# Two transformer layers and a second block on one core: five reordered places and attention scores one unit ahead

## The chip, the cores and the metric

The kernel runs on one core of one Trainium2 chip, in one launch. The metric is the device time in microseconds (us); the median of three runs is taken. The engines are PE (products), DVE (vector), ACT (activations), POOL and SP, of which the last issues nearly all DMAs. Each has a queue of its own, worked in order; they meet at semaphores.

## The reference

One sequence of 256 tokens, model width 1024, fp32, goes through two layers (`first_block`) and a second block:

```python
for l in range(DEPTH):                       # 2
    mod = silu(c) @ w_ada[l] + b_ada[l]      # 1024 x 6144: sh1, sc1, gt1, sh2, sc2, gt2
    h = x * (1.0 + sc1) + sh1
    z = h @ w_in[l] + b_in[l]                # split in aq ak av | bq bk bv bf | cq ck cv cg | gates
    ya = rmsnorm(diff_attention(aq, ak, av, lam))       # A: 4 heads, two softmax maps each
    yb = forgetting_attention(bq, bk, bv, log_sigmoid(bf))   # B: 4 heads
    yc = groupnorm(retention(rotary(cq), rotary(ck), cv)) * silu(cg)   # C: 4 heads
    m = ga * (ya @ w_pa) + gb * (yb @ w_pb) + gc * (yc @ w_pc)
    x = layernorm(ALPHA * x + gt1 * (m @ w_out[l]))
    h = x * (1.0 + sc2) + sh2
    u, g = split(h @ w_up[l])                # 2 x 2816
    x = layernorm(ALPHA * x + gt2 * ((gelu(conv3(u)) * g) @ w_down[l]))
```

The second block (the middle and the expert loop) is a gated delta rule, a SwiGLU, a windowed attention and a mixture of 8 experts of which each token takes 2, each with a residual and a layer norm.

## The kernel before

Every fp32 product is three products of parts: each operand is split in a high part (ACT rounds it, L1482) and a low part (DVE subtracts it, in place, L1871), and `product` issues high x high (L794), low (L795) and high x low (L796). Weights come in slots of 1 MB (128 x 2048) through a ring of four slots `W` that SP fills (L653). `RING_LOADS` lists them by part of the program (layer0, layer1, middle); slot numbers start at 0 in each part. A slot is free when PE has used its low part and, for the high part, there are two slots, so `high(n)` on ACT and `low(n)` on DVE mean: split the next n half-weights. Where they stand in each engine's program sets the order of the work.

The results of PE go to the eight PSUM banks (each 2 KB a partition), handed out as a ring in the order of the jobs (`psum`); a job starts when the one eight places earlier has been copied out. `take_chunk` on DVE copies a finished chunk of z with its bias (L1861), and frees its bank.

The modulation `mod` is made in twelve chunks of 512 columns (`ada`): DVE multiplies weight rows by silu(c) and adds them in 8 steps (L1937, L1939), PE adds the 128 partitions with a product by a matrix of ones (`ada_column`, L922, one column for 128; `ada_row`) and DVE adds the bias (`ada_in`, L2004). Chunks 0 to 3 of layer 0 are made ahead of the first product, chunks 4 to 9 within the six chunks A0 to B2 of z, and 10 and 11 and the chunks of the next layer in `up`, one step (L1964) a tile. `ada_column(c)` waits for the chunk's sum.

A layer runs: hT (transposes of x, scale and shift, split: `shifted`/`high_shifted`), chunks A0 to A2, B0 to B2 and bf, then C and the gates as `background` pieces of the attention loops. There are eight units of A (u = 0 to 7) and eight of B (8 to 15): PE makes the scores (`attend`), DVE masks them and takes the maximum (`mask`, L2139, L2142), ACT the exponentials (L1542), DVE the probabilities (L2312 to L2318), PE transposes them (`attend_T`, L968) and multiplies by v (`attend_out`). Four C heads follow. The mixer's outputs: transposes of yA and yB, products pa and pb, transposes of yC, pc, the gated sum `mix`, its transposes mT, the product with w_out, residual and norm (L2047), then up (22 tiles of 128 hidden columns; the width-3 convolution by three operations, L2119 to L2123, Gelu on ACT, L1576, the gate L2099 and the split L2101 and L2103) and down. After down, the last norm of a layer waits for the split of the next layer's first weights (`high_next`).

## Time and profile before

| | us |
|---|---|
| median of 3 runs | 3078.68 |
| lowest and highest | 3076.17, 3080.14 |
| profiled execution, whole | 3081.78 |
| its span in the trace | 3080.0 |
| layer 0, layer 1 | 0 to 712, 712 to 1364 |
| middle, expert loop | 1364 to 2040, 2040 to 3080 |

The profiled execution is 3.1 us above the median of the runs, 1.8 us of which lie outside its span. In the profile's rows the first number is the start in us from the start of the span, the second the duration in us; "x32" are 32 instructions in one row, and "[9.85 <-DVE arena L1861]" says that the engine stood idle for 9.85 us before it and what ended that. An fp32 product shows as more than one instruction (passes). The mean granted clock of PE is 0.919 of its full speed.

### The profile page before, as it was taken

Reading aid. Unit: us, or ns where it says so; the run is one execution under the profiler, and the core shown is the slowest. Engines: PE = TensorE matmul, PEld = TensorE weight load, DVE = VectorE, ACT = ScalarE, POOL = GpSimd, SP = SyncE. Lnnn points to the kernel's source line nnn. Section 1 sums busy time; section 2 is a strip of 40 time slices with the busy share of each in tenths; the row PEclk is TensorE's granted clock in tenths of the full one; section 3 lists DMA queues with packets and bytes.
Section 4 is the critical chain, followed back from the end, with each engine's and each line's share of the span. In section 5 each row is a group of like instructions: output and inputs, shape, how many; then the busy total and the mean of one; then the engine's idle time right before and its main releaser. Section 6 shows DMA issues by size and latency. Waiting matters only on the chain.

```text
span 3080.0 us, 38153 instructions
## 1 busy us (share of the span) xinstructions
PE 2696.3 (88%) x13946; PEld 2285.4 (74%) x13946; DVE 2236.1 (73%) x2873; ACT 1470.6 (48%) x1685; POOL 24.0 (1%) x46
## 2 busy tenths in 40 slices
PE   4888888996888779968889996769999999999997
PEld 3667768875666669858788975658888888888885
DVE  6766668868656759745576646469889898898987
ACT  2233433323244333325334324447777777777774
POOL 0000000000000000000000000000000000000000
PEclk7889989998899889978999987669999999999998
DMA  7733435566433345432205552239899898898985
GB/s 303 261 130 127 140 137 202 209 239 250 186 135 127 123 165 213 161 113 108 69 15 177 189 207 108 85 121 361 340 350 356 339 367 338 339 362 343 369 338 214
DMA packets 104569, 671.11 MB, mean 218 GB/s; under 512 B 11968, under 2 KB 12096, under 8 KB 26992
## 3 DMA queue, kind: packets, MB, share of 16 engines
q1 hardware_dynamic: 97440, 622.08, 54.1%
q0 software_dynamic: 6992, 47.19, 4.1%
q8 instruction: 87, 1.43, 0.2%
q14 instruction: 50, 0.41, 0.0%
HBM read 665.03 MB, written 4.19 MB: 217 GB/s over the span
## 4 chain that ended last, share of the span: by engine, by line
PE 43%; DVE 24%; PEld 17%; issue 8%; ACT 6%; DMA 2%; PEldq 0%; DVEq 0%; SPq 0%; ACTq 0%
PE bank L794 12%; PE bank L795 12%; PE bank L796 12%; DVE W_low L1871 8%; PEld bank L796 6%; PEld bank L794 5%; PEld bank L795 5%; PE bank L1136 3%; DVE work L1939 2%; ACT W_high L1482 2%; DMA W<-in_w_expert 1%; ACT scores L1542 1%; PE bank L851 1%; PEld bank L1366 1%; DVE arena L1964 1%
## 5 line engine op out<-in xcount | busy, mean ns | idle before, releaser
L1871 DVE TENSOR_TENSOR W_low<-W,W_high 128x1024 fp32r<-128x1024 f32 x426 | 496.0, 1207 | 328.3 <-ACT W_high L1482 321.6
L1482 ACT ACTIVATE W_high<-W 128x1024 fp32r<-128x1024 f32 x426 | 422.1, 1039 | 588.3 <-PE bank L796 284.3
L795 PE MATMUL bank<-W_low,arena_parts 128*128 128x512 f32 x1224 | 482.8, 394 | 0.0
L794 PE MATMUL bank<-W_high,arena_parts 128*128 128x512 f32 x904 | 364.9, 404 | 30.1 <-DVE work L2467 19.8
L796 PE MATMUL bank<-W_high,arena_parts 128*128 128x512 f32 x904 | 358.4, 396 | 0.0
L796 PE MATMUL bank<-hT_high,W_low 128*128 128x256 f32 x1184 | 341.0, 288 | 0.0
L794 PE MATMUL bank<-W_high,hT_high 128*128 128x512 f32 (+3 forms) x744 | 304.2, 409 | 39.7 <-DVE arena L1861 20.9
L794 PE MATMUL bank<-hT_high,W_high 128*128 128x256 f32 x1072 | 312.3, 291 | 11.6 <-DVE arena L1861 8.8
L795 PE MATMUL bank<-W_low,hT_high 128*128 128x512 f32 (+4 forms) x784 | 310.3, 396 | 0.0
L795 PE MATMUL bank<-hT_low,W_high 128*128 128x256 f32 x1072 | 307.3, 287 | 0.0
L796 PE MATMUL bank<-W_high,hT_low 128*128 128x512 f32 (+3 forms) x744 | 294.1, 395 | 0.0
L794 PE MATMUL bank<-arena_parts 128*128 128x512 f32 x672 | 272.4, 405 | 1.9 <-DVE arena_parts L2979 1.9
L795 PEld LDWEIGHTS bank<-W_low,arena_parts 128*128 128x128 f32 x1224 | 233.4, 191 | 47.6
L796 PE MATMUL bank<-arena_parts 128*128 128x512 f32 x672 | 263.5, 392 | 0.0
L796 PEld LDWEIGHTS bank<-hT_high,W_low 128*128 128x128 f32 x1184 | 233.7, 197 | 0.0
L794 PEld LDWEIGHTS bank<-W_high,arena_parts 128*128 128x128 f32 x904 | 173.6, 192 | 69.9 <-issue 22.0
L795 PE MATMUL bank<-arena_parts 128*128 128x512 f32 x576 | 225.2, 391 | 0.0
L1528 ACT ACTIVATE arena_parts<-W 128x2048 fp32r<-128x2048 f32 x96 | 184.3, 1920 | 84.3 <-DMA W<-in_w_expert 66.2
L794 PEld LDWEIGHTS bank<-hT_high,W_high 128*128 128x128 f32 x1072 | 209.7, 196 | 16.4 <-issue 10.9
L1904 DVE TENSOR_TENSOR W_low<-W,arena_parts 128x2048 fp32r<-128x2048 f32 x96 | 217.9, 2283 | 3.4 <-ACT arena_parts L1528 3.4
L795 PEld LDWEIGHTS bank<-hT_low,W_high 128*128 128x128 f32 x1072 | 210.0, 196 | 0.5 <-issue 0.5
L794 PEld LDWEIGHTS bank<-W_high,hT_high 128*128 128x128 f32 x744 | 152.3, 205 | 76.5 <-issue 42.2
(372 smaller groups left out, 4719.1 us busy)
## 6 DMA issues: line engine op xcount, KB each, us to landing
W<-in_w_expert SPq DMA_DIRECT2D x192, 1024.0 KB, 4.8
W<-in_w_layer SPq DMA_DIRECT2D x170, 1024.0 KB, 4.9
arena<-in_w_expert SPq DMA_DIRECT2D x144, 1024.0 KB, 4.8
W<-in_w_middle SPq DMA_DIRECT2D x58, 1024.0 KB, 4.8
arena<-in_w_layer POOLq DMA_DIRECT2D x40, 1024.0 KB, 6.9
R<-in_rows_layer SPq DMA_DIRECT2D x70, 256.0 KB, 6.2
R<-in_rows_middle SPq DMA_DIRECT2D x18, 256.0 KB, 5.8
spread<-arena POOLq DMA_DIRECT2D x1, 3072.0 KB, 12.8
```

Source lines behind the costliest of these rows:

```text
L794: mm(bank, lhs[0], rhs[0], start=start, stop=False)
L795: mm(bank, lhs[0], rhs[1], start=False, stop=False)
L796: return mm(bank, lhs[1], rhs[0], start=False, stop=stop)
L851: last = turn_over(bank[:, i * P:(i + 1) * P], src[:, t, f:f + P], ident)
L1136: last = mm(bank[:, i * P:(i + 1) * P], lhs(i), rhs(i), start=True, stop=True)
L1366: last = turn_over(bank[:, i * P:(i + 1) * P], hid_tok[:, c % 2, i * P:(i + 1) * P], ident)
L1482: do(high_slot(at, w)[:, cols], raw(at, w)[:, cols], ACT.Copy).then_inc(main_highs.filled[main_highs.slot(at, w)], 1)
L1528: do(expert_high(j), expert_raw(j), ACT.Copy).then_inc(stream.raised, 1)
L1542: i = do(scores[:, b, m, 0:K], scores[:, b, m, 0:K], ACT.Exp, bias=nmax[:, b, m:m + 1], accum_out=rsum[:, b, m:m + 1])
L1871: tt(lows(at, w)[:, cols], raw(at, w)[:, cols], high_slot(at, w)[:, cols].bitcast(F32), ALU.subtract).then_inc(*low_ready.event(at))
L1904: tt(expert_low(j), expert_raw(j), expert_high(j).bitcast(F32), ALU.subtract).then_inc(stream.lowered, 1)
L1939: i = stt(acc, part, csil[:, f:f + 1], acc, ALU.mult, ALU.add)
```

## The change

Nothing of what is computed changes, but chunks 0 to 3 of `mod` are made in another way. Six parts:

- **Launch** (layer 0): `ada_first` multiplies the four chunks on PE directly, weight columns stationary, silu(c) moving; two before the transposes of x and two after; DVE only adds. The constants are loaded in two parts, x two weights later, and the two halves of `shifted` have a weight split between them.
- **Sums**: `first_steps` makes the steps of chunks 4 to 9 a generator. Of a chunk's eight steps three stand ahead of `take_chunk`, three (five at A0) behind; the others behind bf and in units 0 to 3 of A. Double steps in `up` are from tile 15 on, and the first column sum of the next layer moves from up's tile 21 to down's first.
- **Attention**: PE's scores, DVE's mask and ACT's exponentials of unit u+1 stand ahead of the probabilities of u.
- **Mixer outputs**: transposes and splits of yA and yB move into the C stage (their buffers from hT to the arena). Order of the products: pa0, pa1, pb0, yC's transposes, pb1, pc0, first half of pc1, first half of mT, rest of pc1, rest of mT, out. `mix` is signalled by tile, not once.
- **Ring slots**: `RING_START` lets the next part go on with the slot after the last one.
- **Convolution**: the first tap is an ACT Identity with scale and bias, the high part of the hidden a copy by ACT, the bank is freed by the gate of j-1, the low part of j-2 comes behind it.

In the middle, splits are moved from between the halves of a residual to behind the shift (and expert slots behind the last one). The counts of `high` and `low` follow. The core of the diff:

```diff
+RING_START = {part: sum(len(RING_LOADS[p]) for p in list(RING_LOADS)[:n]) for n, part in enumerate(RING_LOADS)}
...
-        yATs = hT_high[:, 0:4, :], hT_low[:, 0:4, :]
-        yBTs = hT_high[:, 4:8, :], hT_low[:, 4:8, :]
+        yATs, yBTs = both(7680, 9224, 4, S), both(2048, 3072, 4, S)
...
+            def more_constants():
+                sp.wait_ge(consts_in, 16)
+                sp.dma_start(consts[:, 2 * P:], ins["constants"][:, 2 * P:]).then_inc(consts_in, 16)
...
+                load_all(at, after, None if l else {("ada", 1, 1): first_inputs, ("A", 1, 1): more_constants})
...
-                        pool.wait_ge(*ada_ready.nth(at, 3))
+                        pool.wait_ge(*weights.full(at, ("A", 0, 0)))
...
+            def ada_first(c):
+                pe.wait_ge(*psum.vacant(at, ("ada", c)))
+                bank = banks[psum.slot(at, ("ada", c))]
+                for half in range(2):
+                    w = ("ada", c, half)
+                    pe.wait_ge(*weights.full(at, w))
+                    part = W[:, weights.slot(at, w), :]
+                    for i in range(4):
+                        n = 4 * half + i
+                        for k in range(4):
+                            f = 4 * half + k
+                            a_ = k * 512 + i * P
+                            last = mm(bank[:, n:n + 1], part[:, a_:a_ + P], csil[:, f:f + 1], start=k == 0, stop=k == 3)
+                    if half == 0:
+                        last.then_inc(*weights.frees(at, w))
+                last.then_inc(*psum.fills(at, ("ada", c)))
+                used.append((w, ("ada", c)))
+                hand_back()
...
+                    for c in range(2):
+                        ada_first(c)
...
                     transposes("hT", x, KD, None, 0)
-                    for c in range(4):
-                        ada_column(c)
+                    for c in range(2, 4):
+                        ada_first(c)
                 for n in range(6):
                     kind, c = ("A", n) if n < 3 else ("B", n - 3)
                     run(chunk((kind, c), (kind, c), hTs, KD, 512, 0 if n == 0 else None))
-                    if n:
+                    if n in (1, 3, 4, 5):
                         hand_back()
-                        (ada_row if n < 3 else ada_column)(3 + n)
+                        {1: ada_row, 3: ada_row}.get(n, ada_column)({1: 4, 3: 5, 4: 6, 5: 7}[n])
...
+                scores_a(0)
                 for h_ in range(A_HEADS):
                     for t in range(NT):
-                        attend("A", h_, t, aT[:, h_, :], aT[:, 4 + h_, :], 2)
+                        if u < 7:
+                            scores_a(u + 1)
                         next(bg)
+                        if u == 4:
+                            hand_back()
+                            ada_column(9)
                         attend_T("A", h_, t, u, 1)
...
                 transposes("cT", zCqk, 8, None, 0)
+                transposes("yA", yA, 4, y_ready, 1)
...
+                    if h_ == 1:
+                        transposes("yB", yB, 4, y_ready, 3)
                 for _ in bg:
                     pass
-                transposes("yA", yA, 4, y_ready, 1)
-                transposes("yB", yB, 4, y_ready, 3)
-                for b, (yT, kt) in enumerate(((yATs, 4), (yBTs, 4), (yCTs, 8))):
-                    if b == 2:
-                        transposes("yC", yC, 8, y_ready, 5)
-                    for n in range(2):
-                        run(chunk(("p", b, n), ("p" + "abc"[b], n), yT, kt, 512,
-                                  None if n else (4, 6, 8)[b]))
-                transposes("mT", mix, KD, h_ready, 1, 0)
+                for n in range(2):
+                    run(chunk(("p", 0, n), ("pa", n), yATs, 4, 512, None if n else 4))
+                run(chunk(("p", 1, 0), ("pb", 0), yBTs, 4, 512, 6))
+                transposes("yC", yC, 8, y_ready, 5)
+                run(chunk(("p", 1, 1), ("pb", 1), yBTs, 4, 512))
+                run(chunk(("p", 2, 0), ("pc", 0), yCTs, 8, 512, 8))
+                c = chunk(("p", 2, 1), ("pc", 1), yCTs, 8, 512)
+                next(c)
+                transposes("mT", mix, KD, h_ready, 1, 1, NT, quarters=(0,))
+                run(c)
+                transposes("mT", mix, KD, h_ready, 1, 1, NT, quarters=(1,))
                 for n in range(2):
                     run(chunk(("out", n), ("out", n), mixTs, KD, 512, None if n else 12))
-                transposes("h2T", x, KD, h_ready, 2, 1, NT)
+                transposes("h2T", x, KD, h_ready, 5, 1, NT)
...
-                    if j == 21 and l + 1 < DEPTH:
-                        hand_back()
-                        next_column(0)
                 def between_down(c):
-                    if l + 1 < DEPTH and c in (3, 6, 8):
+                    if l + 1 < DEPTH and c in (0, 3, 6, 8):
...
+            def hidden_conv(n, hid, taps):
+                def copy(j):
+                    act.wait_ge(*hid_mul.nth(a.at, j + 1))
+                    do(hid[0][:, j, :], acted[:, j % 2, :], ACT.Copy).then_inc(*hid_high.event(a.at))
+                for j in range(n):
+                    act.wait_ge(*psum.full(a.at, ("up", j)))
+                    bank = banks[psum.slot(a.at, ("up", j))]
+                    c = work[:, (j % 2) * S:(j % 2 + 1) * S]
+                    do(c, bank[:, 0:S], ACT.Identity, scale=taps[:, 2 * n + j:2 * n + j + 1],
+                       bias=taps[:, 3 * n + j:3 * n + j + 1]).then_inc(*hid_tap.event(a.at))
+                    high(1)
+                    if j:
+                        copy(j - 1)
+                    act.wait_ge(*hid_pre.nth(a.at, j + 1))
+                    if j >= 2:
+                        act.wait_ge(*hid_ready.nth(a.at, j - 1))
+                    do(acted[:, j % 2, :], c, ACT.Gelu).then_inc(*hid_act.event(a.at))
+                    act.wait_ge(*hid_act.last(a.at))
+                copy(n - 1)
...
+                    high_shifted("hT", 8, 0, lambda q: high(1))
...
+            def first_steps():
+                for c in range(4, 10):
+                    acc = work[:, c % 2 * 512:c % 2 * 512 + 512]
+                    if c > 5:
+                        dve.wait_ge(*psum.full(v.at, ("ada", c - 2)))
+                    for f in range(KD):
+                        w = ("ada", c, f // 4)
+                        if f % 4 == 0:
+                            dve.wait_ge(*adas.full(v.at, w))
+                        part = ada_slots[:, adas.slot(v.at, w), f % 4 * 512:(f % 4 + 1) * 512]
+                        if f == 0:
+                            i = ts(acc, part, csil[:, 0:1], None, ALU.mult)
+                        else:
+                            i = stt(acc, part, csil[:, f:f + 1], acc, ALU.mult, ALU.add)
+                        i.then_inc(dve_done, 1)
+                        dve.wait_ge(dve_done, v.count())
+                        if f % 4 == 3:
+                            dve.nop().then_inc(*adas.frees(v.at, w))
+                        if f == KD - 1:
+                            dve.nop().then_inc(*ada_ready.event(v.at))
+                        yield
...
+                if c < 4:
+                    tt(m, bank[:, 4:8], m, ALU.add).then_inc(dve_done, 1)
+                    dve.wait_ge(dve_done, v.count())
...
+                def gate(j):
+                    dve.wait_ge(*hid_act.nth(v.at, j + 1))
+                    bank = banks[psum.slot(v.at, ("up", j))]
+                    whole = acted[:, j % 2, :]
+                    tt(whole, whole, bank[:, S:2 * S], ALU.mult).then_inc(*hid_mul.event(v.at))
+                    dve.wait_ge(*hid_mul.last(v.at))
+                    dve.nop().then_inc(*psum.frees(v.at, ("up", j)))
+                def rest(j):
+                    dve.wait_ge(*hid_high.nth(v.at, j + 1))
+                    tt(hid[1][:, j, :], acted[:, j % 2, :], hid[0][:, j, :].bitcast(F32), ALU.subtract
+                       ).then_inc(*hid_ready.event(v.at))
+                    dve.wait_ge(*hid_ready.last(v.at))
                 for j in range(n):
-                    dve.wait_ge(*psum.full(v.at, ("up", j)))
+                    low(1)
+                    dve.wait_ge(*hid_tap.nth(v.at, j + 1))
                     u = banks[psum.slot(v.at, ("up", j))]
                     c = work[:, (j % 2) * S:(j % 2 + 1) * S]
-                    low(1)
-                    ts(c, u[:, 0:S], taps[:, 2 * n + j:2 * n + j + 1], taps[:, 3 * n + j:3 * n + j + 1], ALU.mult, ALU.add).then_inc(dve_done, 1)
-                    dve.wait_ge(dve_done, v.count())
                     stt(c[:, 1:S], u[:, 0:S - 1], taps[:, n + j:n + j + 1], c[:, 1:S], ALU.mult, ALU.add).then_inc(dve_done, 1)
                     dve.wait_ge(dve_done, v.count())
                     stt(c[:, 2:S], u[:, 0:S - 2], taps[:, j:j + 1], c[:, 2:S], ALU.mult, ALU.add).then_inc(*hid_pre.event(v.at))
                     dve.wait_ge(*hid_pre.last(v.at))
                     if j:
-                        finish_hidden(j - 1, hid, True)
+                        gate(j - 1)
+                    if j > 1:
+                        rest(j - 2)
                     between(j)
-                finish_hidden(n - 1, hid, True)
+                gate(n - 1)
+                rest(n - 2)
+                rest(n - 1)
...
                     low(1)
-                    ada(4 + n, 0)
+                    sums(3)
                     low(1)
-                    ada(4 + n, 1)
                     take_chunk(kind, c, lambda t: z[:, t, c * 512:(c + 1) * 512], ready)
-                    if n:
-                        ada_in(3 + n)
+                    if n in (1, 3, 4, 5):
+                        ada_in({1: 4, 3: 5, 4: 6, 5: 7}[n])
+                    sums(3 if n else 5)
...
+                mask_a(0)
                 for u in range(8):
                     h_, t = divmod(u, NT)
                     K, b = (t + 1) * P, u % 2
-                    mask("A", h_, t, u, 2, A_DQK ** -0.5, lambda m, K: blocks[:, 2 * P - K:2 * P])
+                    if u < 7:
+                        mask_a(u + 1)
                     dve.wait_ge(*exped.nth(v.at, u + 1))
...
+                    if u < 4:
+                        sums(2)
                     if u == 2:
                         log_forget()
+                    if u == 4:
+                        fold(32, 40, 16, 24, 64)
...
+                dve.wait_ge(*gate_done.nth(v.at, 2))
+                for n in range(2):
+                    gated(0, n)
+                low_tiles("yC", 2, yCTs)
+                low(1)
+                dve.wait_ge(*gate_done.nth(v.at, 3))
+                gated(1, 0)
+                low(1)
+                gated(1, 1)
+                low(1)
+                dve.wait_ge(*gate_done.nth(v.at, 4))
+                gated(2, 0, h_ready)
+                low(1)
+                low_tiles("mT", 1, mixTs)
+                low(1)
+                gated(2, 1, h_ready)
+                low_tiles("mT", 2, mixTs, 1)
+                low(1)
                 low(2)
                 residual(outs("out")[0:2], 0, ALPHA)
-                low(2)
+                low(1)
...
                 residual(outs("out")[2:4], 0, ALPHA)
                 norm(h_ready)
-                shifted("h2T", modc[:, 64:72], modc[:, 72:80])
+                shifted("h2T", modc[:, 64:72], modc[:, 72:80], lambda q: low(q))
...
-                    for _ in range(2 if j > 9 and j % 2 else 1):
+                    for _ in range(2 if j > 13 and j % 2 else 1):
...
             residual(outs("gout")[0:2], None, ALPHA)
-            low(2)
+            low(1)
             residual(outs("gout")[2:4], None, ALPHA)
             norm(h_ready)
-            shifted("fxT", modc[:, 0:8], modc[:, 8:16])
+            shifted("fxT", modc[:, 0:8], modc[:, 8:16], lambda q: low(q))
...
             low(1)
-            lower_slot(0, 1)
-            lower_slot(0, 2)
             residual(outs("wout")[2:4], None, ALPHA)
             norm(h_ready)
             shifted("mxT", modc[:, 32:40], modc[:, 40:48])
+            lower_slot(0, 1)
+            lower_slot(0, 2)
```

## Rows read from the trace of the kernel before

**Rows 1.** Part 1 of the page: busy us (share of span) x instructions.

```profile
PE 2696.3 (88%) x13946; PEld 2285.4 (74%) x13946; DVE 2236.1 (73%) x2873; ACT 1470.6 (48%) x1685; POOL 24.0 (1%) x46
```

**Rows 2.** PE's waits over the span: total us, times, longest us.

```profile
PE bank L851 <- DVE x L2047: 79.0, 7, 20.4
PE bank L794 <- DVE arena L1861: 29.7, 6, 9.8
...
PE bank L968 <- DVE scores L2318: 25.3, 12, 4.7
...
PE bank L968 <- DVE small L2385: 19.1, 8, 4.8
```

**Rows 3.** Timeline of PE at launch: start, us, engine, line, operation [idle before <-releaser].

```profile
19.50 0.95 PE L922 MATMUL bank<-consts,work 128*128 128x1 f32 x8
28.24 1.87 PE L922 MATMUL bank<-consts,work 128*128 128x1 f32 x8 [7.79 <-DVEq L1947]
...
50.99 0.76 PE L794 MATMUL bank<-W_high,hT_high 128*128 128x512 f32 x1 [7.76 <-DVE hT_low L1898]
```

**Rows 4.** Timeline of DVE at launch: seven of the eight sum operations.

```profile
7.00 5.59 DVE L1939 SCALAR_TENSOR_TENSOR work<-W,small,work 128x512 f32<-128x512 f32 x7
```

**Rows 5.** Timeline of PE in the middle: products of one column.

```profile
1437.82 5.53 PE L1171 MATMUL bank<-consts,arena 128*128 128x1 f32 x32 [0.33 <-PE bank L796]
```

**Rows 6.** Timeline of PE, layer 0, chunk bf: 4-column products (48 in a row).

```profile
142.18 0.25 PE L794 MATMUL bank<-W_high,hT_high 128*128 128x4 f32 x1
...
142.49 0.35 PE L796 MATMUL bank<-W_high,hT_low 128*128 128x4 f32 x1
```

**Rows 7.** Timeline of DVE, layer 1, chunk B0.

```profile
772.93 2.36 DVE L1871 TENSOR_TENSOR W_low<-W,W_high 128x1024 fp32r<-128x1024 f32 x2
775.21 3.10 DVE L1939 SCALAR_TENSOR_TENSOR work<-arena,small,work 128x512 f32<-128x512 f32 x4
778.64 1.53 DVE L1861 TENSOR_TENSOR arena<-bank,R 128x512 f32<-128x512 f32 x2 [0.32 <-DVE work L1939]
```

**Rows 8.** Timeline of PE, layer 1, behind chunk B0.

```profile
779.47 0.77 PE L794 MATMUL bank<-W_high,hT_high 128*128 128x512 f32 x1 [9.85 <-DVE arena L1861]
```

**Rows 9.** Timeline of PE, layer 0, attention A.

```profile
195.16 0.69 PE L968 MATMUL bank<-consts,scores 128*128 128x128 f32 x2 [4.67 <-DVE scores L2318]
```

**Rows 10.** Timeline of DVE, layer 0, attention A.

```profile
173.49 0.17 DVE L2312 RECIPROCAL small<-small 128x2 f32<-128x2 f32 x1 [1.37 <-ACT scores L1542]
```

**Rows 11.** Timeline of PE, layer 0, mixer outputs.

```profile
369.30 1.97 PE L851 MATMUL bank<-consts,arena 128*128 128x128 f32 x8 [3.68 <-DVEq L2426]
...
409.21 0.77 PE L794 MATMUL bank<-W_high,arena_parts 128*128 128x512 f32 x1 [9.90 <-DVE work L2467]
...
441.76 0.47 PE L794 MATMUL bank<-W_high,arena_parts 128*128 128x512 f32 x1 [3.50 <-DVEq L1921]
```

**Rows 12.** Timeline of DVE, layer 0, norm of yC.

```profile
375.33 1.76 DVE L2442 TENSOR_SCALAR arena<-arena,small 128x256 f32<-128x256 f32 x4 [0.25 <-DVE hT_low L1918]
```

**Rows 13.** Timeline of DVE, layer 0, up.

```profile
507.43 2.36 DVE L1871 TENSOR_TENSOR W_low<-W,W_high 128x1024 fp32r<-128x1024 f32 x2
509.71 0.54 DVE L2119 TENSOR_SCALAR work<-bank,taps_kept 128x256 f32<-128x256 f32 x1
...
513.35 1.23 DVE L1871 TENSOR_TENSOR W_low<-W,W_high 128x1024 fp32r<-128x1024 f32 x1
```

**Rows 14.** Timeline of PE, ends of layer 0 and layer 1.

```profile
711.86 0.90 PE L851 MATMUL bank<-consts,x 128*128 128x128 f32 x3 [20.39 <-DVE x L2047]
...
1363.83 0.90 PE L851 MATMUL bank<-consts,x 128*128 128x128 f32 x3 [18.37 <-DVE x L2047]
```

**Rows 15.** Timeline of ACT, end of layer 0.

```profile
694.87 2.00 ACT L1482 ACTIVATE arena_parts<-W 128x1024 fp32r<-128x1024 f32 x2 [14.02 <-DMA W<-in_w_layer]
```

**Rows 16.** Timeline of PE, the longest norm wait of the middle.

```profile
2010.25 0.69 PE L851 MATMUL bank<-consts,x 128*128 128x128 f32 x2 [10.81 <-DVE x L2047]
```

**Rows 17.** Timeline of DVE, in the last residual of the middle.

```profile
2001.55 4.49 DVE L1904 TENSOR_TENSOR arena_parts<-arena,arena_parts 128x2048 fp32r<-128x2048 f32 x2
```

255 lines of the change are left out of this document (129 added, 126 removed).

## The prediction

> **What bounds the kernel now.** The page's first part comes first: PE, the engine of the products, is busy 88% of the span, more than any other [rows 1]. So the end moves by two things only, by PE's idle time (12%, some 360 us) and by the clock at which its products run. The second view is the list of PE's waits, which says what ended the idle time [rows 2]: the seven norms that hold the next stage's transposes cost 79.0 us, the copies of a finished chunk out of its bank (L1861) 29.7, the two attention loops 25.3 and 19.1. The third is the timeline around each long wait, to see what stood in DVE's queue ahead of the instruction that PE waited for. The rows below come from there. The expert loop, from about 2040 us to the end, holds less than 5 us of PE's idle time and is not edited. All the change can do lies ahead of it, in two layers (0 to 712, 712 to 1364) and the middle.
>
> **Launch, layer 0.** Removed: DVE's sums of the first eight weight slots. A slot is one operation of 0.48 us and seven others that with it fill two slots of four (the row of 5.59 us is seven of them) [rows 4], and after each chunk PE adds the 128 rows with eight passes [rows 3]. Added: each of the four chunks is multiplied on PE, 2 halves x 4 columns x 4 parts = 32 fp32 products with a result of one column, 64 passes as the profile counts them (a column sum of four products is its x8 row), so 256 in all. Their price hangs on the clock. Eight such passes took 0.95 us right after the transposes, and 1.87 us after an idle of 7.79 us: 0.12 us each at the upper level (2.4 GHz), 0.22 at the lower (1.2 GHz) [rows 3]. Which level will a stretch of 256 of them have? The middle shows 32 passes of one column following full-width products with only 0.33 us of idle: they take 5.53 us, 0.17 each, a mean between the two levels [rows 5]. The bias chunk of B's gate is the same with four columns: product after product without a gap, and while the record at 142.18 us is 0.25 us long, those from 142.49 on take 0.35 [rows 6]. So narrow products lose the upper level while PE is never idle. I take the lower level for all 256: 256 x 0.2225 = 57 us, less some 3 us for those right after the transposes, which keep the level of [rows 3]. First weight half on chip at about 6.5 us, where DVE begins now [rows 4]: two chunks to 35.3, transposes to 38.8, the third chunk to 50.3, the fourth to 64.5, then the add of the column, the shift of hT and its split, 5.4 us as today (the last column sum ends near 43.2, first product 50.99, of which 2.4 us were a weight split that now lies earlier). First product at 69.9 instead of 50.99 [rows 3]: **+19 us**. At the upper level the passes are 256 x 0.119 = 30.4 us, and then DVE, the loads and the shift set the start, near 47.5: -3.5 us.
> The Trainium skill ("TensorE: Matmul & The Clock Gate", "Part 1: The HAM clock gate") says that the clock gate rewards a TensorE kept continuously busy. By that the new stream of unbroken products would have the full clock, and the launch would be worth the -3.5 us. Rows 5 and 6 speak against it: the engine was continuously issuing there and lost the level.
>
> **Sums of the ada chunks.** Behind chunk B0 PE stands 9.85 us in each layer until a bank is copied out [rows 8]. DVE's queue at that point is low, four steps, low, four steps, and only then the copy: 2.36, 3.10, 2.36, 3.10 and 1.53 us [rows 7]. Now three of the steps stand ahead of the copy, the others behind it. Ahead of the copy of B0 8 steps become 3, at 0.775 us: 3.9 us directly, and the two chunk sums that PE no longer waits for (4 and 5 go behind A1 and B0) 1 us each. I follow the chain from the first product to the end of C's first half: B0 starts 1.8 earlier, B1 8.0 earlier with some 3.5 of idle left, the end 8.4 earlier. Twice: **-17 us**, from 0 (the steps that are moved return as a wait of T0) to -20 (all of 9.85).
>
> **Attention.** PE's transposes of the probabilities wait for DVE: 25.3 us in A and 19.1 in B over both layers [rows 2], with one wait of 4.67 us [rows 9]. DVE itself waits 1.37 us for ACT's exponentials in a unit [rows 10]. Scores, mask and exponential of unit u+1 ahead of the probabilities of u take out that trip through ACT, about 1.1 us in each of the 7 later units of A and of B. In A that is 7.7 us less two ada steps (1.55 us) in each of the first four units, of which PE's own work (7.2 to 7.9 us a unit) hides half: -4.6. That long wait stays since it comes from extra DVE work (logarithm of the gate, spread) that is not moved. In B PE waits for over 1 us in three units alone: -3.3. A layer -7.9, both -15.8, of which I take **-15 us**. Bounds: 0 and the whole 44 us.
>
> **Mixer outputs.** Today: transposes of yA and yB behind C's last head with an idle of 3.68 us, products, the transposes of yC and then 9.90 us until DVE has taken the banks of p, 3.50 before the output's products [rows 11]. With yA and yB inside the C stage, their idle and 2 us of transposes go off the path (C's heads are PE-bound, so the 4 us of transposes count there: C ends 2 later). pb0 needs a bank, and DVE gives back pa's only after the norm of yC (its blocks of 1.75, 1.42, 1.23 us [rows 12]): about 3 us of idle at yC. The 9.90 becomes 2.4, the 1.64 and 3.50 together 1.5, since half of the transposes of mix stand between the halves of pc1. Sum per layer: 3.7+1.3-2 from the head, 9.9-5.4 in the middle, 1.6+3.5-1.5 at the end, and 5 us from the weight splits that no longer stand ahead of the copies, 16 us: **-32 us** both. Bounds -38 and, if DVE's queue behind the norm of yC is the true limit, -12. The split of low(2) behind the last norm of this stage: its row of 7.20 becomes some 4.4, **-6 us** both.
>
> **Convolution.** DVE's loop in up is 5.92 us a tile with one ada step: low at 507.43, the next at 513.35 [rows 13], and PE needs 5.8. The first tap (0.54 [rows 13]) and the cast go to ACT: DVE's own work is 5.0, or 5.8 with a double step. But now a loop runs tap (ACT) -> high (ACT) -> low -> two taps (DVE) -> gate -> copy -> gelu (ACT), which I add up to 6.25 us a tile only in part overlapped. I take up at the pace of PE where DVE was late (the tiles with two steps) and no gain elsewhere: -5 a layer. In layer 0 the first column sum of the next layer waits for steps that now come later, some +2.5: **-7 us** both. Bounds -18 and +4.
>
> **Ring.** Between layers PE stands 20.39 and 18.37 us [rows 14]. In the first, ACT has waited 14.02 us for the weight's DMA: the first weight of the next layer goes to slot 0, which is freed by one of the last down weights [rows 15]. With the ring carried on (layer 0 has 90 loads, so layer 1 begins in slot 2; 82 more, so the middle begins in 0, next in line), both loads can go two weights earlier, before the down products end. The residual then starts at PE's last bank, 687.5 instead of 701.75: PE at 697.3 instead of 711.86: -14.5. The middle's start the same way, -12.5. **-27 us**. What is late next is the norm's own chain, 6 us. If another wait holds SP (the queue is in order), 0.
>
> **Middle.** Of the seven norm waits the longest here is 10.81 us [rows 16]. Ahead of it two expert slots are split between two halves of the residual, a row of 4.49 us [rows 17]; they go behind the shift, where DVE has 5 us free beside the router's weights: -4.6. One low (2.36) each goes out of two residual chains: **-8 us** in all, 0 if the steps return in the routing chain.
>
> **The sum.** +19 - 17 - 15 - 32 - 6 - 7 - 27 - 8 = -93 us, on the profiled execution's 3081.8: 2988.8. The median of the runs shown is 3.1 us below that execution, so 2986.
>
> **Rivals.**
> 1. *The clock stays up at launch* (the rule above): 2986 - 22.5 = 2963.5. For it: the first eight passes behind transposes were at the upper level [rows 3]. Against it: rows 5 and 6. Chance 0.15.
> 2. *DVE hands the gains on*: DVE is second with 73% and its work is hardly less; where PE comes earlier, it meets DVE's queue (mixer at its bound, -12 instead of -32, attention and sums at half, -16 instead of -32, up 0, norm and middle at half, -7): launch +19, ring -27: -43 us, 3036. Chance 0.22. If only the ring does not do what it says (SP held elsewhere), 3013: chance 0.05.
> 3. *The convolution's loop becomes serial* (the other side). Of the loop's eight steps, none overlaps with the next tile's: 0.45 + 2.01 + 2.36 + 0.96 + 0.42 + 0.40 + 0.43 + 0.75 + 0.42 = 8.2 us a tile instead of 5.92, 44 tiles: +100 us, so 2986 + 107 = 3093. It decides from 8.0 us a tile on, and only if nothing of the other stages is better than forecast. Against it: in the row of now ACT's next high starts before DVE's work is through. Chance 0.04.
> The forecast has the rest, 0.54. Less than 2 in 10 is left out by a range from 2950 (the clock up and the terms at their better ends) to 3035. A measurement of this kernel tells some 0.2%, 6 us, from no change: faster 0.95, same 0.01, slower 0.04.
>
> **What would show it.** Launch: rows of one-column passes at 0.22 each (right) or 0.12 (rival 1), first full-width product near 70 us. Sums: the wait on L1861 behind B0 at 3 to 4 us instead of 9.85. Attention: waits on the probabilities down by a third. Mixer: the idle of 9.90 gone, one of 3 at yC instead. Up: 136 to 142 us in each layer; above 150 is rival 3. Layer ends: 20.39 and 18.37 become about 6. Wrong altogether I would be if PE's idle time shrinks by less than 60 us, or if PE's records at the lower level grow outside the launch.

## The result, and the profile after

| | before | after |
|---|---|---|
| median of the runs, us | 3079.41 (4 runs) | 3031.39 (4 runs, 3030.18 to 3032.69) |
| ratio to before | | 0.9842, 95% interval 0.9825 to 0.9859 |
| span of the profiled execution | 3080.0 | 3028.6 |
| mean granted clock of PE | 0.919 | 0.933 |

The change is worth 48 us where 93 were forecast, 1.6% of the time. The time lies in the range of 2950 to 3035, near its upper end. The page's first part and PE's list of waits for the changed kernel (total us, times, longest):

```profile
PE 2732.2 (90%) x14170; PEld 2319.9 (77%) x14170; DVE 2177.5 (72%) x2757; ACT 1508.3 (50%) x1773; POOL 24.4 (1%) x46
```

```profile
PE bank L862 <- DVE x L2130: 36.4, 7, 9.1
PE bank L805 <- DVE W_low L1953: 26.5, 34, 5.5
...
PE bank L999 <- DVE small L2497: 19.0, 8, 3.9
PE bank L999 <- DVE scores L2423: 17.6, 10, 3.3
PE bank L805 <- DVE arena L1943: 15.9, 6, 4.7
PE bank L1106 <- DVE arena_parts L2001: 14.0, 2, 7.0
...
PE bank L805 <- DVE arena_parts L2001: 9.8, 2, 4.9
```

Against [rows 2]: the norms' waits fell from 79.0 to 36.4 us and those for a chunk's bank (now L1943) from 29.7 to 15.9, as forecast. Of the two attention lists the one of A fell by a third, 25.3 to 17.6, as forecast, and the one of B did not move, 19.1 to 19.0. And 23.8 us stand there that no line of before had: PE waits for the splits of yA and yB (L2001), four times.

A table by stage says where the time went. Each stage runs from one named product of PE to the next in both traces (A from its first transposed probabilities to its last, and B likewise), and the forecast stands beside it. Each number is that of one traced execution.

| stage (both layers where there are two), us | before | after | moved | forecast |
|---|---|---|---|---|
| launch, to the first full-width product | 50.99 | 68.58 | +17.6 | +19 |
| chunks, to the first transposed probabilities | 115.28 + 117.91 | 107.06 + 109.58 | -16.6 | -17 |
| attention A (u 0 to 7) | 67.66 + 66.61 | 65.80 + 66.97 | -1.5 | -9 |
| between A and B | 16.15 + 16.15 | 18.31 + 18.29 | +4.3 | (part of A and B) |
| attention B | 67.66 + 69.11 | 62.28 + 65.10 | -9.4 | -6 |
| C, mixer outputs and norm | 155.40 + 154.26 | 149.64 + 148.76 | -11.3 | -38 |
| up and down | 218.34 + 209.56 | 220.71 + 210.34 | +3.2 | -7 |
| layer ends | 20.38 + 18.37 | 9.11 + 5.65 | -24.0 | -27 |
| middle and experts | 1716.2 | 1702.4 | -13.8 | -8 |

The sum of the moves is -51.4 us, which is the difference of the spans. Three stages explain most of the gap of 42 us to the forecast: the mixer's outputs (27), attention (8) and up (10); the layer ends add 3, and the middle was 6 better. The launch, the mixer outputs, A, up and the ends have runs below.

The launch, PE's timeline of the changed kernel (start, us, then the operation):

```profile
6.87 13.79 PE L939 MATMUL bank<-small,W 128*128 128x1 f32 x64 [6.87 <-DMA W<-in_w_layer]
20.96 13.78 PE L939 MATMUL bank<-small,W 128*128 128x1 f32 x64 [0.30 <-PE bank L939]
35.05 3.64 PE L862 MATMUL bank<-consts,x 128*128 128x128 f32 x16 [0.31 <-PE bank L939]
38.49 10.55 PE L939 MATMUL bank<-small,W 128*128 128x1 f32 x64
49.34 13.78 PE L939 MATMUL bank<-small,W 128*128 128x1 f32 x64 [0.30 <-PE bank L939]
68.58 0.79 PE L805 MATMUL bank<-W_high,hT_high 128*128 128x512 f32 x1 [5.46 <-DVE W_low L1953]
```

64 passes take 13.78 us, 0.215 each, close to the passes of [rows 3] after an idle. Only the chunk right behind the transposes is shorter, 10.55 us. The first product comes at 68.58, forecast 69.9.

The waits of the C stage and the DVE rows that lead up to the first of them, layer 0:

```profile
347.64 1.70 PE L1106 MATMUL bank<-arena 128*128 128x256 f32 x4 [7.01 <-DVE arena_parts L2001]
...
372.39 0.77 PE L805 MATMUL bank<-W_high,hT_high 128*128 128x512 f32 x1 [4.92 <-DVE arena_parts L2001]
```

```profile
342.34 2.36 DVE L1953 TENSOR_TENSOR W_low<-W,W_high 128x1024 fp32r<-128x1024 f32 x2 [2.74 <-ACT W_high L1535]
344.62 0.42 DVE L2532 BATCH_NORM_STATS2 small<-bank 128x6 f32<-128x256 f32 x1
...
346.89 0.69 DVE L2001 TENSOR_TENSOR arena_parts<-bank,arena_parts 128x512 fp32r<-128x512 f32 x1
```

PE has transposed yA into two banks by 326.3 us (its row of transposes starts at 323.52 and takes 2.78). DVE empties them at 346.89, behind a weight split that itself waited 2.74 us for ACT (whose Silu and Sigmoid of the gates, the latter 1.91 us at 339.31, stand ahead of its own part of that split) and behind the statistics of head 0. Until then PE has no bank, for 7.01 us.

The ends of the layers, against [rows 14]:

```profile
701.49 0.90 PE L862 MATMUL bank<-consts,x 128*128 128x128 f32 x3 [9.11 <-DVE x L2130]
...
1326.18 1.11 PE L862 MATMUL bank<-consts,x 128*128 128x128 f32 x4 [5.66 <-DVE x L2130]
```

### The profile page after: what moved, and what is told of

Same layout as the page of the kernel before. It is cut to its first block, busy times and chain, and to the rows that moved or that the text cites. A ratio compares the mean times of both kernels' runs of the same rounds, so it can differ in the third digit from the quotient of the medians.

```text
span 3028.6 us, 38615 instructions
## 1 busy us (share of the span) xinstructions
PE 2732.2 (90%) x14170; PEld 2319.9 (77%) x14170; DVE 2177.5 (72%) x2757; ACT 1508.3 (50%) x1773; POOL 24.4 (1%) x46
## 4 chain that ended last, share of the span: by engine, by line
PE 43%; DVE 21%; PEld 17%; issue 8%; ACT 7%; DMA 3%; PEldq 0%; DVEq 0%; ACTq 0%; SPq 0%
PE bank L805 12%; PE bank L806 11%; PE bank L807 11%; DVE W_low L1953 7%; PEld bank L807 5%; PEld bank L805 5%; PEld bank L806 5%; ACT W_high L1535 3%; PE bank L1189 3%; PE bank L939 2%; DMA W<-in_w_expert 2%; PE bank L862 1%; DVE work L2020 1%; PEld bank L1419 1%; DVE scores L2235 1%
## 5 line engine op out<-in xcount | busy, mean ns | idle before, releaser
L806 PE MATMUL bank<-W_low,arena_parts 128*128 128x512 f32 x1288 | 506.5, 393 | 0.0
L805 PE MATMUL bank<-W_high,arena_parts 128*128 128x512 f32 x968 | 388.3, 401 | 10.1 <-DVE W_low L1953 5.8
L807 PE MATMUL bank<-W_high,arena_parts 128*128 128x512 f32 x968 | 381.9, 395 | 0.0
L805 PE MATMUL bank<-W_high,hT_high 128*128 128x512 f32 (+3 forms) x680 | 280.6, 413 | 35.6 <-DVE W_low L1953 12.1
L806 PE MATMUL bank<-W_low,hT_high 128*128 128x512 f32 (+4 forms) x720 | 286.1, 397 | 0.0
L806 PEld LDWEIGHTS bank<-W_low,arena_parts 128*128 128x128 f32 x1288 | 244.4, 190 | 49.2
L807 PE MATMUL bank<-W_high,hT_low 128*128 128x512 f32 (+3 forms) x680 | 270.1, 397 | 0.0
L805 PEld LDWEIGHTS bank<-W_high,arena_parts 128*128 128x128 f32 x968 | 184.4, 191 | 53.0 <-DVE W_low L1953 8.8
L807 PEld LDWEIGHTS bank<-W_high,arena_parts 128*128 128x128 f32 x968 | 183.8, 190 | 40.1
## 6 DMA issues: line engine op xcount, KB each, us to landing
spread<-arena POOLq DMA_DIRECT2D x1, 3072.0 KB, 13.7
```

The costliest lines, as they stand in the source:

```text
L805: mm(bank, lhs[0], rhs[0], start=start, stop=False)
L806: mm(bank, lhs[0], rhs[1], start=False, stop=False)
L807: return mm(bank, lhs[1], rhs[0], start=False, stop=stop)
```

## The experiments

Every ratio is to the kernel before, run on the same chip. Where a time is set against the changed kernel's 3031.39, the chips can differ; the kernel before took 3078.0 to 3080.8 us on the three that were used. Single stages are read from each run's trace, one execution each. PE's clock puts 2 to 5 us of scatter into a stage that no edit touches (last section), and the stretch from the middle on, which none of the ten runs edits (only e4 moves its ring slots), took 1697.2 to 1707.6 us. So a part of a few us is believed where its stage is steady over the runs, and not from the whole time, nor from one trace of a stage that is not steady.

**e1, launch back on DVE.** Is the launch's cost what it seems, or had its earlier loads paid something back?

```diff
-                    for c in range(2, 4):
-                        ada_first(c)
+                    for c in range(4):
+                        ada_column(c)
...
+                    for c in range(1, 4):
+                        ada(c, 0)
+                        ada(c, 1)
+                        ada_in(c - 1)
```

> The changed kernel with its launch taken back: chunks 0 to 3 of the modulation are summed by DVE again, constants and x are loaded as before; all other edits stay. In the changed kernel the first full-width product starts at 68.58 us instead of 50.99. My theory: the launch edit costs those 17.6 us and nothing later gives them back, so this run takes 3031 - 17.6 = 3014 us, with the first product at 51.0. Rival: the earlier weight splits and loads of the new launch had paid a part back in the first chunks: 3020 to 3026.

Measured: 3016.98 us, ratio 0.979 (0.9774 to 0.9807). The first product stands at 50.98, so the launch is 17.6 us shorter. Against 3031.39 the whole is 14.4 less, and by the ratios (0.9842 - 0.979) x 3080 = 16 us. In the trace nothing is missing up to the end of the layers, where this run stands 18.6 us ahead of the changed kernel; 5.2 us are lost behind it, in the middle and the experts (1707.6 us instead of 1702.4), which the edit does not touch. The launch edit costs what the forecast said.

**e2, the splits of yA and yB earlier in DVE's queue.** Is it their place that holds the banks, or is DVE simply late in the C stage?

```diff
+                low_tiles("yA", 1, yATs)
                 low(1)
                 for h_ in range(C_HEADS):
...
-                    if h_ == 0:
-                        low_tiles("yA", 1, yATs)
-                    if h_ == 2:
+                    if h_ == 1:
                         low_tiles("yB", 1, yBTs)
```

> The changed kernel with DVE's split of yA moved from behind C's first head to ahead of its first weight split, and that of yB from behind the third head to behind the second. PE stands 7.01 and 4.92 us a layer there, waiting for a bank that these splits free. My theory: the place in DVE's queue is the cause, so both waits go in both layers: 3031 - 24 = 3007 us, and some us less where PE's clock no longer falls behind them. Rival: DVE as a whole is late in the C stage, and the idle time comes back at yC's norm or at the products of p: 3022 us or more.

Measured: 3009.49 us, ratio 0.9771 (0.9755 to 0.9788), 22 us less than the changed kernel. The traced execution was the fastest of the four (2999.2 us, the others 3007.6 to 3014.9). C, mixer and norm take 135.63 and 135.45 us instead of 149.64 and 148.76: -27.3 us, and e8, e9 and e10, which have the same edit, show 26.9 to 28.3. The four waits on L2001 are gone from the list of waits. DVE has the splits done in time it had been idle in:

```profile
328.18 0.69 DVE L2001 TENSOR_TENSOR arena_parts<-bank,arena_parts 128x512 fp32r<-128x512 f32 x1 [1.61 <-ACT arena_parts L1574]
329.09 0.69 DVE L2001 TENSOR_TENSOR arena_parts<-bank,arena_parts 128x512 fp32r<-128x512 f32 x1 [0.22 <-DVE arena_parts L2001]
333.59 2.36 DVE L1953 TENSOR_TENSOR W_low<-W,W_high 128x1024 fp32r<-128x1024 f32 x2 [3.81 <-ACT W_high L1535]
```

Even behind them DVE waits 3.81 us. So the cause was the order alone, and the 27.3 us are the forecast's missing 27. They are not the 23.8 of the waits plus a rest: PE's idle time in the two stages fell by 18.4 us (49.4 to 30.9), since shorter waits came in the place of the four, such as 2.42 us ahead of the product pc0. The other 9 us go with the clock: full-width products at the lower level cover 8.5 us there instead of 23.7, and such a product starts every 0.43 us at the lower level and every 0.23 at the upper. With the splits early the stage is 38.6 us shorter than before; the forecast had 38.

**e3, the ada steps out of attention A.** The steps moved into A's first four units, against the emptied trip through ACT.

```diff
-                    sums(3 if n else 5)
+                    sums(3 if n in (1, 2) else 5)
...
-                sums(2)
+                sums(4)
...
-                    if u < 4:
-                        sums(2)
```

> The changed kernel with the eight ada steps of attention A's units 0 to 3 put into the chunk stage instead (behind the copies of A0, B0, B1, B2 and behind bf). Attention A gained 0.4 us a layer at most where I forecast 4.5. Theory: the 6.2 us of steps fill what scores one unit ahead had emptied, so without them A shortens by 4 to 6 us a layer and the chunk stage lengthens by at most 2: 3021 to 3027 us. Rival: A is held by PE's clock after its short waits (16.0 us at the lower level in layer 1 instead of 7.1), or by the logarithm and spread, and nothing moves: 3029 to 3033.

Measured: 3029.27 us, ratio 0.9834 (0.9817 to 0.985). By the whole time this is no difference from the changed kernel. In its trace A takes 59.02 and 60.96 us instead of 65.80 and 66.97 (-12.8 for both), the chunk stages 108.21 and 114.18 instead of 107.06 and 109.58, and the launch, which the edit doesn't touch, 71.79 instead of 68.58. A's longest wait at u = 3 fell from

```profile
203.41 0.69 PE L999 MATMUL bank<-consts,scores 128*128 128x128 f32 x2 [3.26 <-DVE scores L2423]
```

to 1.67 us. But in layer 1 a wait came back at the end of the chunks, where the changed kernel has 0.30 us:

```profile
812.87 0.47 PE L999 MATMUL bank<-consts,scores 128*128 128x128 f32 x1 [4.59 <-DVE scores L2423]
```

That is the lower bound which the prediction gave for the sums: "the steps that are moved return as a wait of T0". And one trace is too few here. Six kernels have the steps in A and four have them out, with the same code otherwise in these two stages (layer 0 and 1 added, us):

| | chunk stages | attention A | both |
|---|---|---|---|
| steps in A (changed kernel, e1, e2, e4, e5, e7) | 216.2 to 221.1, mean 218.3 | 130.6 to 132.8, mean 132.0 | mean 350.3 |
| steps out (e3, e8, e9, e10) | 222.4 to 228.1, mean 224.4 | 120.0 to 128.7, mean 124.3 | mean 348.8 |

So DVE's queue held A, and without the eight steps (6.2 us a layer) A is 7.7 us shorter for both layers, of which e3's 12.8 is the best case. The chunk stages are 6.2 us longer, so that no gain is left that these traces could show. The whole time had said so.

**e4, the weight ring restarted at slot 0.**

```diff
-RING_START = {part: sum(len(RING_LOADS[p]) for p in list(RING_LOADS)[:n]) for n, part in enumerate(RING_LOADS)}
+RING_START = {part: 0 for part in RING_LOADS}
```

> The changed kernel with the weight ring starting again at slot 0 in each layer and in the middle. Theory: the layer ends' waits return from 9.11 and 5.66 us to some 20 and 18: 3031 + 24 = 3055 us. Rival: part of the shorter ends comes from elsewhere (splits that the norms wait for), then +8 to +15, 3039 to 3046.

Measured: 3055.82 us, ratio 0.9918 (0.9902 to 0.9935), 24.4 more than the changed kernel. The ends are back:

```profile
716.34 0.90 PE L862 MATMUL bank<-consts,x 128*128 128x128 f32 x3 [20.50 <-DVE x L2130]
```

```profile
1353.70 3.68 PE L862 MATMUL bank<-consts,x 128*128 128x128 f32 x16 [18.37 <-DVE x L2130]
```

The shorter ends come from the slots alone, all 24 us of them.

**e5, the convolution back on DVE** (the functions `hidden` and `hidden_conv` of ACT and DVE as before).

```diff
-                hidden_conv(FF1 // P, hid1, taps_kept)
+                hidden(FF1 // P, ACT.Gelu, True)
```

> The changed kernel with the convolution as before: first tap and cast on DVE, bank given back and low part made with the gate of j-1. In the changed kernel a tile takes 6.1 us where 5.9 was needed before, and up is 1.9 and 0.9 us longer than before instead of 5 shorter. Theory: the trip between ACT and DVE (tap, split, taps, gate, copy, gelu) is one serial loop of 6.1 us, so this run has up at 143 to 147 us a layer, 0 to 8 us less in all: 3024 to 3031. Rival: the ada steps that now stand later in up are what is late, and up stays as long or gets longer without the relief of DVE: 3031 to 3040.

Measured: 3034.15 us, ratio 0.9853 (0.9836 to 0.9871), which by the whole time is no gain. Up, with the transposes ahead of it, takes 145.36 and 144.64 us instead of 149.54 and 147.93: -7.5 us. What takes it back stands in stages that this edit does not touch: the launch +3.3, layer 1's chunks +4.8 us and, behind the layers, +2.1. Up itself is steady: in the eight traces with this convolution on ACT it takes 149.2 to 150.2 us in layer 0, and e9 repeats the gain. The rows show the loop. The changed kernel's DVE and ACT in up, one tile apart:

```profile
518.16 2.36 DVE L1953 TENSOR_TENSOR W_low<-W,W_high 128x1024 fp32r<-128x1024 f32 x2 [1.37 <-ACT W_high L1535]
...
522.49 0.75 DVE L2044 SCALAR_TENSOR_TENSOR arena<-arena,small 128x512 f32<-128x512 f32 x1
524.54 2.36 DVE L1953 TENSOR_TENSOR W_low<-W,W_high 128x1024 fp32r<-128x1024 f32 x2 [1.30 <-ACT W_high L1535]
```

```profile
521.92 0.42 ACT L1634 ACTIVATE arena_parts<-acted 128x256 fp32r<-128x256 f32 x1 [2.92 <-DVE acted L2199]
522.55 0.42 ACT L1648 ACTIVATE acted<-work 128x256 f32<-128x256 f32 x1 [0.21 <-DVE arena_parts L2205]
523.00 0.56 ACT L1640 ACTIVATE work<-bank,taps_kept 128x256 f32<-128x256 f32 x1
523.47 2.00 ACT L1535 ACTIVATE W_high<-W 128x1024 fp32r<-128x1024 f32 x2
528.31 0.42 ACT L1634 ACTIVATE arena_parts<-acted 128x256 fp32r<-128x256 f32 x1 [2.85 <-DVE acted L2199]
```

and DVE's in e5:

```profile
511.93 2.36 DVE L1934 TENSOR_TENSOR W_low<-W,W_high 128x1024 fp32r<-128x1024 f32 x2
517.85 2.36 DVE L1934 TENSOR_TENSOR W_low<-W,W_high 128x1024 fp32r<-128x1024 f32 x2
```

6.38 us from split to split in the changed kernel (6.46 in most tiles), 5.92 in most tiles of e5, where DVE waits for nothing. (Some tiles, those with two steps above all, take 6.1 to 8.7 us in e5, so the gain over 22 tiles is 4.2 and 3.3 us a layer and not 22 x 0.5.) In the changed kernel ACT waits 2.9 us for the gate, then copies, makes the Gelu, the tap and the high part one after the other, and DVE waits 1.3 us for the first half of that high part: each engine waits for the other once a tile. The ada step (the row at 522.49) and the second half of the high part run beside the other engine. The moved work made DVE idle, not PE faster.

**e6, scores not ahead** (scores, mask and exponentials of unit u in unit u again, A and B).

```diff
-                        if u < 7:
-                            scores_a(u + 1)
+                        scores_a(u)
...
-                    if u < 7:
-                        mask_a(u + 1)
+                    mask_a(u)
```

> The changed kernel with PE's scores, DVE's mask and ACT's exponentials of a unit back in that unit, for A and B. With the sums out of A's units (run e3) A fell by 6.8 and 6.0 us, so the ahead order and those sums work against each other. Theory: without it A is longer by 5 to 7 us a layer (the steps stay in it) and B by 3 to 4: 3031 + 18 = 3049 us. Rival: A was never held by the trip through ACT, and only B grows: 3037 to 3040.

Measured: 3048.75 us, ratio 0.9906 (0.9885 to 0.9926), 17.4 more. A grows by 8.0 and 5.9 us, B by 5.4 and 2.3, and the stretch between A and B shrinks by 2.0 and 2.1, which is the first unit's chain, that has to run ahead of B's first unit. So one unit ahead is worth some 17 us for both layers. The change shows 6.6 for attention, since e6's attention is itself 10.8 us longer than that of the kernel before: A, which now holds eight steps in each layer, takes 146.7 us for both instead of 134.3. These 12.4 us are the full price of the steps, 2 x 8 x 0.775.

**e7, wide products between the one-column ones**, a probe of PE's clock. It adds work and leaves none out.

```diff
                         for k in range(4):
...
+                        last = mm(bank[:, P:4 * P], part[:, 0:P], part[:, 0:3 * P], start=True, stop=True)
```

> A probe of PE's clock: the changed kernel with one more product of 384 columns behind every four one-column products of the launch (32 more in all, their results in bank columns that nothing reads). Theory: the one-column products are what the clock does not hold for. With wide ones between them, the one-column passes fall from 0.215 us to some 0.12 us and the wide products run at the upper level. Rival: the launch is slow for another reason (the stationary operand is loaded anew for each product, or the clock is low in this stretch whatever is run): the passes stay at 0.215 us.

Measured: 3050.21 us, a single execution. Both theories fail. PE's timeline ahead of the transposes of x and behind them:

```profile
52.56 1.71 PE L939 MATMUL bank<-small,W 128*128 128x1 f32 x8
54.13 1.63 PE L940 MATMUL bank<-W 128*128 128x384 f32 x2
56.06 3.46 PE L862 MATMUL bank<-consts,x 128*128 128x128 f32 x16 [0.30 <-PE bank L940]
59.35 0.95 PE L939 MATMUL bank<-small,W 128*128 128x1 f32 x8
60.17 0.89 PE L940 MATMUL bank<-W 128*128 128x384 f32 x2
...
82.97 0.95 PE L939 MATMUL bank<-small,W 128*128 128x1 f32 x8
83.78 0.89 PE L940 MATMUL bank<-W 128*128 128x384 f32 x2
```

Ahead of the transposes the same mixture stays at the lower level (1.2 GHz) for 49 us, half of PE's time being wide products. Behind them it stays at the upper level (2.4 GHz) for 25 us, to its end: eight passes in 0.95 us, where the changed kernel's fell back within the first chunk. So in this execution the mixture did not raise the level, but kept it, and the changed kernel's one-column products alone did not keep it. The reloading of the stationary operand does not set the pace, since at the upper level the same passes take 0.12 us each.

**e8, the launch on DVE, both y splits early, steps out of A** (the edits of e1, e2 and e3 together).

> Launch on DVE as before, the splits of yA and yB early, and the ada steps out of A's units; all other edits as in the changed kernel. By the stages of the earlier runs the parts add: -17.6 (launch), -27.3 (waits for a bank in the C stage), -12.8 (A) and +1 to +5 in the chunk stage: 3031 - 54 = 2977 us. Rival: the gains overlap, since the earlier C stage and the earlier A meet the same queue of DVE: 2990 or more.

Measured: 2988.44 us, ratio 0.9708 (0.9693 to 0.9723), 43 us faster than the changed kernel. The mixer keeps its gain (134.34 and 135.81 us) and the launch too (50.89). A has 64.38 and 64.36, only 4 us less in all than the changed kernel, and layer 1's chunks 114.37. Eleven us of the expected sum are missing, 8.8 of them in A; most of the rest is in the chunk stages, which grew by 6.9 where 1 to 5 were expected. In A it is not the idle time: that is 6.6 us in layer 0 in e8 and 6.9 in e3, against 10.7 in the changed kernel. But the records of full-width products at the lower level cover 14.5 us of the stage in e8 and 4.9 in e3, and a us at that level holds about half the work: 4.8 us, of a difference of 5.4. Layer 1 is the same (14.4 against 8.6). So in A the rival of overlapping gains is not it; the expectation had taken e3's -12.8, which had the better clock, for the price of the steps.

**e9, e8 with the convolution on DVE** (e5's edit).

> The kernel of run e8 (2988 us) with the convolution on DVE as in the kernel before. Run e5 showed up shorter by 4.2 and 3.3 us, though its whole time was not better, since other stretches fell in a longer clock phase. Theory: the loop of 6.46 us a tile between ACT and DVE goes, and the time falls by 7 us to 2981. Rival: the gain of up is within what the clock's phases give and take: 2986 to 2990.

Measured: 2982.11 us, ratio 0.9692 (0.9674 to 0.971). Up is 4.6 and 2.7 us shorter than in e8 (145.51 and 145.73), the whole 6.3 (4.9 by the ratios). The intervals overlap, so the whole time alone does not show the gain; the stage does.

**e10, e9 with the copy of ada chunk 10 at tile 14 of up.**

```diff
-                    if j == 17:
+                    if j == 14:
                         ada_in(10)
```

> The kernel of run e9 with the copy of ada chunk 10 out of its bank at tile 14 of up instead of 17. PE waits 4.7 and some 3.4 us there in every kernel so far, for the bank of a chunk whose sum was ready three tiles ahead. Theory: the waits go, 7 us less than e9: 2974. Rival: the copy now stands ahead of DVE's own tile and holds up the gate, or the wait is for another bank: as e9.

Measured: 2979.47 us, ratio 0.9679 (0.9664 to 0.9694). Up takes 139.11 and 140.32 us instead of 145.51 and 145.73: the wait of e9

```profile
560.33 0.55 PE L798 MATMUL bank<-hT_high,W_high 128*128 128x256 f32 x1 [5.31 <-DVE arena L1914]
```

is gone, and the idle time ahead of the next layer's first column sum, in down, grew from 4.20 to 6.50 us, since the sum's steps are DVE's and have not become earlier:

```profile
597.72 1.86 PE L963 MATMUL bank<-consts,arena 128*128 128x1 f32 x8 [6.50 <-DVEq L2047]
```

Of the 11.8 us that up gained, 2.8 went into layer 0's down. Another 8.3 were lost in layer 0's chunks and A (112.22 for 108.22, 63.15 for 58.85), which come earlier than the edit: a wait of 3.68 us at the first transposed probabilities where e9 has 0.30, and in A more of the lower level. By the whole time e10 and e9 cannot be told apart. e10, at 0.968 of the kernel before, has the lowest median of the study: 52 us below the changed kernel.

## Why the prediction was right in direction and twice too large

**Launch: right.** +19 forecast, +17.6 measured, and e1 gives the same 17.6 back. The step that carried it, that narrow products lose the upper level, taken from [rows 5, 6], holds: 0.215 us a pass. Rival 1 (the clock stays up, -22.5) fell. The Trainium skill ("TensorE: Matmul & The Clock Gate", "Part 1: The HAM clock gate") states that the clock follows how busy TensorE has been. Taken to mean that unbroken work gets the full clock, this would by the forecast's estimate have made the launch 21 us shorter than it is. The trace disagrees where the work is one-column products: 64 passes at a time, with 0.30 us of idle between two chunks, ran at the lower level, but for the start of the chunk behind the transposes.

**Sums: right, but not free.** -17 forecast, -16.6. The wait behind B0 fell from 9.85 to 4.09 us in layer 1 and 3.29 in layer 0, forecast 3.5. Part of the gain is a loan: eight steps a layer stand in attention A instead, and they are priced below.

**Mixer outputs: the failed step.** "With yA and yB inside the C stage, their idle and 2 us of transposes go off the path": I priced PE's work that moves (4 us) and not the banks it takes along. Two banks each stay full until DVE has split them, and I did not look where in DVE's queue those splits had been put: behind a weight split that waits for ACT, behind the statistics of a head. That cost 7.01 and 4.92 us in each layer, 23.8 in waits, and e2 gives back 27.3 with the clock: in size this is the whole of the term's error (38 forecast, 11.3 measured). Of the other steps of the term e2 shows the 9.90 us as 2.42 (forecast 2.4), yC's wait as 1.5 (forecast 3) and the norm's 7.20 as 4.92 (forecast 4.4). That the stage with the splits early is 38.6 us shorter, against the 38, is partly luck: the term named idle time only, and PE's idle time fell by 29.0 us (59.9 to 30.9). The rest goes with the clock, which the sum held constant: full-width products at the lower level cover 8.5 us of the two stages instead of 29.1.

**Attention: mis-sized.** -15 forecast, -6.6 measured. The term was 7.7 us a layer for the trip through ACT in A, less 3.1 for the ada steps, and 3.3 in B. B gave 4.7 a layer, more than forecast. A gave 0.7 a layer instead of 4.6. For both layers A took 134.3 us before, and 124.3 in the mean of the four kernels with the new order and no steps in it: the order is worth 10 us there, where I had counted 15.4, and this is the larger error. The steps cost 7.7 in the new order (132.0 instead of 124.3), where I had 6.2, so that letting PE's own work hide half of them was nearly right; in the old order they would have cost 12.4 (e6). Nor had I the 2.1 us a layer between A and B, where B's first scores, mask and exponential now run with nothing beside them. "Bounds: 0 and the whole 44" held.

**Convolution: wrong sign.** -5 a layer forecast, +1.9 and +0.9 measured, and e5 shows the edit itself at about +3.7 a layer. I had added the loop up to 6.25 us and then called it "only in part overlapped", without a row for it. It is 6.46 us a tile and serial. This is rival 3 (the loop becomes serial) at 0.5 us a tile rather than 2.3: the mechanism came in at a quarter of its price. Rival 3's sum of 8.2 us counted the ada step (0.75) and the second half of high (1.0) one after the other with the rest, and the rows above show both beside it: 8.2 - 0.75 - 1.0 is 6.45.

**Ring: right.** -27 forecast, -24.0, and e4 returns 24.1. The end of layer 0 kept 9.11 us where I gave it 6.

**Middle: better than forecast.** -13.8 instead of -8. The norm wait of [rows 16] fell from 10.81 to 6.41 us, and another from 10.69 to 2.67, where the term held 2.4. No run takes this part alone, and with the scatter of 1697.2 to 1707.6 over the edited kernels it could as well be read as -9 or -19.

**Rival 2** (DVE hands the gains on, 3036) came nearest to the time, and by luck: it had the mixer at -12 since DVE was said to be late, and e2 shows DVE idle there. Its 3036, with a chance of 0.22, lay outside the range up to 3035 that was said to leave out less than 2 in 10.

The share of PE's time at the lower level is the last piece. My sum had the clock as it was in each stage. Attention A of layer 1 has 11.2 us at the lower level after and 7.6 before, at 2.1 us less idle time, which gives nearly all of it back. Neither sign of being wrong altogether came: PE's idle time shrank by 87 us (383.7 to 296.4), and full-width products at the lower level outside the launch cover 134 us after and 138 before. One reading of the prediction was off without harm: from 2040 us on PE's waits come to 15.3 us in the trace before and not to less than 5, 8.6 of them in one that ends at 2043.5; nothing was edited there.

## What to carry to other kernels

When work is moved earlier on one engine, follow what it holds (banks, slots, buffers) to the instruction that frees it, and read what stands ahead of that one in its own queue: the splits of yA and yB cost 24 us in waits for being a few instructions too late. Moving work from the busier engine to the idler one pays only if it leaves no new round trip: add up the loop across the engines and compare it with the pace of the engine that bounds. When steps are moved from one stage to another, price both stages: e3's steps left A 7.7 us shorter and the chunks 6.2 longer. And test an edit smaller than the scatter of the whole time by its stage, but in more than one trace: up's gain was 7.5 us in e5 and 7.3 in e9 and can be believed, while e3's 12.8 was not found again.

## What the runs showed of the hardware that was not expected

The same instructions don't get the same clock each time. The launch's chunk right behind the transposes took 10.55 us in the changed kernel and some 13.7 in e3, and the first full-width product stood at 68.6 us in two kernels and at 71.7 to 72.1 in four, with no edit ahead of it. In e3 it is

```profile
38.59 13.65 PE L939 MATMUL bank<-small,W 128*128 128x1 f32 x64
```

Layer 1's chunks take 109.6 to 110.5 us in the changed kernel, e1 and e7, and 112.5 to 114.4 in e2, e4 and e5, whose code is the same there. For the attention stage, from records of full-width products over 0.5 us long:

| attention A, layer 0, us | length | idle | at the lower level |
|---|---|---|---|
| before | 67.7 | 13.0 | 9.0 |
| after | 65.8 | 10.7 | 9.1 |
| e2 | 65.1 | 11.7 | 5.7 |
| e3 | 59.0 | 6.9 | 4.9 |
| e8 | 64.4 | 6.6 | 14.5 |
| e9 | 58.8 | 6.9 | 4.8 |
| e10 | 63.2 | 7.1 | 13.6 |

e3, e8, e9 and e10 have the same order of instructions there and nearly the same idle time, and differ by up to 5.5 us. e9 shows both within one execution: 58.85 us in layer 0 and 63.30 in layer 1, with 4.8 and 15.3 us at the lower level. What sets which of the two it is was not found; the stages ahead end at other points of time, and that is all the traces tell.

The second is e7: in its one execution a mixture of narrow and wide products kept whichever level PE already had, the lower for 49 us and the upper for 25. The level rose behind the sixteen transposes of x (3.46 us) that stand between. In the kernel before it was already at the upper level behind the same transposes, though PE had stood idle for 16.10 us ahead of them: the eight passes behind them took 0.95 us. But this is not certain either. In the changed kernel and e2 the passes behind the transposes began at the upper level, and in e3 to e6, with the same instructions up to there, they did not (13.65 us for 64). So what a stretch gets depends on what ran ahead of it and not on its own products alone, and even that did not settle it.
